# The latents' two norms and their split in one stage, and the final norm taken into the second block's first projection

## The reference, cut to what matters

```
def rmsnorm(x, g):
    xf = x.astype(F32)
    y = xf * lax.rsqrt(jnp.mean(xf * xf, axis=-1, keepdims=True) + RMS_EPS)
    return (y * g.astype(F32)).astype(x.dtype)

# the latent attention: two latents of 384 and 256 channels
qa, kva, kr = split(h @ mla_w_down)         # kva and kr for all 768 tokens
q  = rmsnorm(qa_lat, mla_q_norm) @ mla_w_uq      # 512 tokens
kv = rmsnorm(kva, mla_kv_norm) @ mla_w_ukv       # 768 tokens
...
# between the blocks
x = rmsnorm(x_lat, final_norm)              # end of the first block
h = rmsnorm(x, norm_mix_w_2)                # start of the second
proj = h @ w_in_2
...
x = x + merged @ w_out_2                    # x is used again here
```

## Time and profile before

| | |
|---|---|
| median of 3 runs | 3406.04 us |
| the profiled execution's own time | 3397.14 us |
| its span, first to last instruction | 3395.4 us |
| PE busy | 2957.6 us, 87% of the span |
| DVE busy | 1685.6 us, 50% |
| ACT busy | 1222.3 us, 36% |
| mean granted TensorE clock | 0.934 of full |

### The profile page before, as it was taken

How to read it: one execution, slowest core, us unless ns; L and a number is a source line. 1 busy time by engine, 2 the same in 40 slices (tenths; PEclk the granted TensorE clock), 3 DMA queues, 4 the chain that set the end, 5 groups by cost and what they waited for, 6 DMA issues and landing times. The chain is left out here.

```text
span 3395.4 us, 37900 instructions
## 1 busy us (share of the span) xinstructions
PE 2957.6 (87%) x14151; PEld 2324.7 (68%) x14151; DVE 1685.6 (50%) x2322; ACT 1222.3 (36%) x1630; POOL 164.6 (5%) x131
## 2 busy tenths in 40 slices
PE   6898998799999999867999999979757878599996
PEld 2384586687888888745777887757635567477775
DVE  1344432734767443435644433342466453588886
ACT  0321131423232232433424442244324322377774
POOL 0000000200011000000000000000000100212110
PEclk9999998899999999989999999989869788799998
DMA  6510010021345242110012222123100023599986
GB/s 245 194 50 13 32 44 26 1 87 67 123 145 170 71 137 93 38 39 21 1 48 89 93 93 75 62 75 93 44 0 1 1 68 131 187 351 349 348 335 238
DMA packets 76310, 362.77 MB, mean 107 GB/s; under 512 B 13428, under 2 KB 17347, under 8 KB 50596
## 3 DMA queue, kind: packets, MB, share of 16 engines
q1 hardware_dynamic: 62404, 327.69, 27.2%
q0 software_dynamic: 13792, 33.58, 3.0%
HBM read 360.68 MB, written 16.27 MB: 111 GB/s over the span
## 5 line engine op out<-in xcount | busy, mean ns | idle before, releaser
L305 PE MATMUL ps<-rounded,rounded 128*128 128x512 f32 (+3 forms) x3700 | 1377.2, 372 | 134.6 <-DVE rounded L2033 24.1
L306 PE MATMUL ps<-rounded,rounded 128*128 128x512 f32 (+3 forms) x3700 | 1338.0, 362 | 0.0
L307 PE MATMUL ps<-rounded,rounded 128*128 128x512 f32 (+3 forms) x3700 | 1335.4, 361 | 0.0
L305 PEld LDWEIGHTS ps<-rounded,rounded 128*128 128x128 f32 (+1 forms) x3700 | 706.4, 191 | 310.6 <-issue 100.0
L307 PEld LDWEIGHTS ps<-rounded,rounded 128*128 128x128 f32 (+1 forms) x3700 | 707.1, 191 | 107.5
L306 PEld LDWEIGHTS ps<-rounded,rounded 128*128 128x128 f32 (+1 forms) x3700 | 708.2, 191 | 95.2
L284 DVE TENSOR_TENSOR rounded<-work,rounded 128x1024 fp32r<-128x1024 f32 (+3 forms) x224 | 306.4, 1370 | 839.4 <-ACT rounded L280 839.3
L280 ACT CAST rounded<-work 128x1024 fp32r<-128x1024 f32 (+3 forms) x224 | 260.9, 1166 | 728.3 <-PE ps L307 640.2
L3181 DVE TENSOR_TENSOR rounded<-work,rounded 128x2048 fp32r<-128x2048 f32 x138 | 311.7, 2288 | 92.8 <-ACT rounded L3029 90.3
L3029 ACT CAST rounded<-work 128x2048 fp32r<-128x2048 f32 x138 | 258.5, 1908 | 85.5 <-PE ps L307 85.5
L291 PE MATMUL ps<-cst 128*128 128x256 f32 x432 | 122.3, 446 | 83.7 <-PEq L171 83.7
(11 more groups left out here) (439 smaller groups left out, 2545.7 us busy)
## 6 DMA issues: line engine op xcount, KB each, us to landing
work<-in_moe SPq DMA_DIRECT2D x138, 1024.0 KB, 7.3
work<-in_ffn_up SPq DMA_DIRECT2D x44, 1024.0 KB, 4.8
work<-in_ffn_down SPq DMA_DIRECT2D x66, 512.0 KB, 3.3
work<-in_ada_w SPq DMA_DIRECT2D x12, 2048.0 KB, 8.7
work<-in_ada_w POOLq DMA_DIRECT2D x48, 512.0 KB, 4.1
work<-in_w_out SPq DMA_DIRECT2D x16, 512.0 KB, 3.6
work<-in_w_gates SPq DMA_DIRECT2D x16, 512.0 KB, 3.6
work<-in_w_in_hy SPq DMA_DIRECT2D x12, 512.0 KB, 3.3
```

Source lines behind the costliest of these rows:

```text
L305: k.nc.tensor.matmul(out, sh, mh, start=start, stop=False)
L306: k.nc.tensor.matmul(out, sh, ml, start=False, stop=False)
L307: return k.nc.tensor.matmul(out, sl, mh, start=False, stop=stop)
```

## The change

`normalise` is gone. `latent_norms` does both latents' norms and their split in one stage, with the method of `Norm`: squares on ACT, tile sums on DVE, column sums on PE, two short roots (128x4 and 128x6), one short reciprocal, 10 diagonals, 10 spreading matmuls. Scaling and gain are one DVE instruction (line 692 of the new kernel), the high parts follow on ACT, and the low parts follow on DVE after all scaling.

`NormOfNorm` replaces the step `final` and the `Norm` of the `w_qk_2` projection. From one pass over `x` it makes two sums, of the squares of x and of the squares of x times the final gain; the first gives the final norm's inverse root, and the second times that inverse squared gives the mean square that the second norm needs. Each tile is scaled once by the product of both inverses. When the last low part is made, DVE writes the 8 tiles of `x` (normalised by the final norm alone, which the residual of the second block needs), and only then comes to the low parts of the next weights. The PSUM rooms of the norms inside `project_act` move: the sums from bank 6 to bank 3 and the matmuls of `keep_running` from bank 7 to bank 0.

```diff
+class NormOfNorm(Norm):
...
+        self.weighted = k.h
+        self.second_columns = sums_at[:, 8:8 + self.n]
+        self.first_inverse, self.mean = (k.made[:, at:at + self.n] for at in (16, 24))
+        self.first_diagonal = k.h_top[:, DT - 2, :]
...
+    def square(self, act):
+        for kk in range(DT):
+            self.k.nc.scalar.activation(self.part(self.squares, kk), self.part(self.k.x, kk), ACT.Square).then_inc(self.squared, 1)
+            self.k.nc.scalar.activation(self.part(self.weighted, kk), self.part(self.k.x, kk), ACT.Square,
+                                        scale=self.first_gain(kk)).then_inc(self.squared, 1)
+
+    def add(self, dve):
+        self.totals = self.part(self.squares, 0), self.part(self.weighted, 0)
+        for kk in range(1, DT):
+            dve.wait_ge(self.squared, 2 * kk + 2)
+            if kk > 1:
+                dve.wait_ge(self.added, 2 * kk - 2)
+            for total, squares in zip(self.totals, (self.squares, self.weighted)):
+                self.k.nc.vector.tensor_tensor(total, total, self.part(squares, kk), ALU.add).then_inc(self.added, 1)
...
+    def sum_and_spread(self, pe):
+        keep_running(k, 20, self.spare)
+        pe.wait_ge(self.added, 2 * DT - 2)
+        for squares, columns in ((self.squares, self.columns), (self.weighted, self.second_columns)):
+            for a in range(self.n):
+                last = k.nc.tensor.matmul(columns[:, a:a + 1], self.part(squares, 0)[:, a * P:a * P + P], k.cst[:, ONE:ONE + 1],
+                                          start=True, stop=True)
+        last.then_inc(self.summed, 1)
+        keep_running(k, 6, self.spare)
+        for n, (spread, diagonal) in enumerate(((self.spread, self.diagonal), (self.first_spread, self.first_diagonal))):
+            for a in range(self.n):
...
+                at = self.t0 + a * P
+                k.nc.tensor.matmul(spread[:, at:at + P], k.cst[:, ONE:ONE + 1].to_broadcast([P, P]), diagonal[:, at:at + P],
+                                   start=True, stop=True).then_inc(self.spread_done, 1)
+        keep_running(k, 4, self.spare)
...
+    def shift(self, act):
...
+        act.wait_ge(self.summed, 1)
+        k.nc.scalar.activation(self.root, self.columns, ACT.Sqrt, bias=k.const("eps"), scale=1.0 / D).then_inc(self.rooted, 1)
+        act.wait_ge(self.mean_made, 1)
+        k.nc.scalar.activation(self.root, self.mean, ACT.Sqrt, bias=k.const("eps"), scale=1.0 / D).then_inc(self.second_rooted, 1)
...
+    def scale(self, dve):
...
+        dve.wait_ge(self.rooted, 1)
+        link(V.reciprocal(self.first_inverse, self.root))
+        link(V.tensor_tensor(self.mean, self.second_columns, self.first_inverse, ALU.mult))
+        V.tensor_tensor(self.mean, self.mean, self.first_inverse, ALU.mult).then_inc(self.mean_made, 1)
+        dve.wait_ge(self.second_rooted, 1)
+        link(V.reciprocal(self.inverse, self.root))
+        link(V.tensor_tensor(self.inverse, self.inverse, self.first_inverse, ALU.mult))
+        for diagonal, inverse in ((self.diagonal, self.inverse), (self.first_diagonal, self.first_inverse)):
+            for a in range(self.n):
+                at = self.t0 + a * P
+                V.tensor_scalar(diagonal[:, at:at + P], k.const("ident"), inverse[:, a:a + 1], None, ALU.mult).then_inc(self.drawn, 1)
+        dve.wait_ge(self.spread_done, 2 * self.n)
+
+        def scale(kk):
+            if kk < DT:
+                V.scalar_tensor_tensor(out=self.part(k.h, kk), in0=self.part(k.x, kk), scalar=self.first_gain(kk),
+                                       in1=self.spread[:, self.t0:T], op0=ALU.mult, op1=ALU.mult).then_inc(self.scaled, 1)
+
+        scale(0)
+        scale(1)
+        for kk in range(DT):
+            dve.wait_ge(self.rounded, kk + 1)
+            V.tensor_tensor(self.part(k.h_pair.low, kk), self.part(k.h, kk), self.part(k.h_pair.high_plain, kk),
+                            ALU.subtract).then_inc(self.ready, 1)
+            scale(kk + 2)
+        dve.wait_ge(self.scaled, DT)
+        for kk in range(DT):
+            x = self.part(k.x, kk)
+            V.scalar_tensor_tensor(out=x, in0=x, scalar=self.first_gain(kk), in1=self.first_spread[:, self.t0:T],
+                                   op0=ALU.mult, op1=ALU.mult).then_inc(self.kept, 1)
+
+
+def latent_norms(k, x, norms):
...
+        def _(pe):
+            keep_running(k, 12, 6)
+            done = 0
+            for tiles, t0, count, at, gain, pair, spread in todo:
+                done += len(tiles) - 1
+                pe.wait_ge(added, done)
+                for a in range(count):
+                    last = nc.tensor.matmul(sums[:, at + a:at + a + 1], squares[:, tiles[0], t0 + a * P:t0 + a * P + P],
+                                            k.cst[:, ONE:ONE + 1], start=True, stop=True)
+                last.then_inc(summed, 1)
+            keep_running(k, 3, 6)
+            for tiles, t0, count, at, gain, pair, spread in todo:
+                for a in range(count):
+                    pe.wait_ge(drawn, at + a + 1)
+                    last = nc.tensor.matmul(spread[:, t0 + a * P:t0 + a * P + P], k.cst[:, ONE:ONE + 1].to_broadcast([P, P]),
+                                            diagonal[:, (at + a) * P:(at + a + 1) * P], start=True, stop=True)
+                last.then_inc(spread_done, 1)
+            keep_running(k, 12, 6)
+
+        @block.scalar
...
+                for n in tiles:
+                    nc.scalar.activation(squares[:, n, t0:T], x[:, n, t0:T], ACT.Square).then_inc(squared, 1)
+            for m, (tiles, t0, count, at, *_) in enumerate(todo):
+                act.wait_ge(summed, len(todo))
+                nc.scalar.activation(root[:, at:at + count], sums[:, at:at + count], ACT.Sqrt, bias=k.const("eps"),
+                                     scale=1.0 / (P * len(tiles))).then_inc(rooted, 1)
+            done = 0
+            for tiles, t0, count, at, gain, pair, spread in todo:
...
+        def _(dve):
+            seen = adds = 0
+            for tiles, t0, *_ in todo:
+                total = squares[:, tiles[0], t0:T]
+                for j, n in enumerate(tiles):
+                    seen += 1
+                    if j:
+                        dve.wait_ge(squared, seen)
+                        if j > 1:
+                            dve.wait_ge(added, adds)
+                        V.tensor_tensor(total, total, squares[:, n, t0:T], ALU.add).then_inc(added, 1)
+                        adds += 1
+            dve.wait_ge(rooted, len(todo))
+            V.reciprocal(inverse, root).then_inc(inverted, 1)
+            dve.wait_ge(inverted, 1)
+            for a in range(columns):
+                V.tensor_scalar(diagonal[:, a * P:(a + 1) * P], k.const("ident"), inverse[:, a:a + 1], None,
+                                ALU.mult).then_inc(drawn, 1)
+            parts = []
+            for m, (tiles, t0, count, at, gain, pair, spread) in enumerate(todo):
+                dve.wait_ge(spread_done, m + 1)
+                for j, n in enumerate(tiles):
+                    V.scalar_tensor_tensor(out=x[:, n, t0:T], in0=x[:, n, t0:T], scalar=gain(j), in1=spread[:, t0:T],
+                                           op0=ALU.mult, op1=ALU.mult).then_inc(scaled, 1)
+                    parts.append((pair, j, n, t0))
+            for done, (pair, j, n, t0) in enumerate(parts):
+                span = slice(t0 - pair.shift, T - pair.shift)
+                dve.wait_ge(rounded, done + 1)
+                V.tensor_tensor(pair.low[:, j, span], x[:, n, t0:T], pair.high_plain[:, j, span], ALU.subtract)
+
...
-def normalise(k, gain_of, shift_of, segs, dst=None, x=None, kt=DT, root_of=D, pair=None):
...
-def project_act(k, weights, dst, func, bias, segs, kt=DT, x=None, norm=None, then=None):
+def project_act(k, weights, dst, func, bias, segs, kt=DT, x=None, norm=None, then=None, first_norm=False):
...
-    norm = Norm(k, *norm, segs, k.pair(2), k.bank(6), 7) if norm else None
+    if norm:
+        kind, more = (NormOfNorm, (k.pair(3),)) if first_norm else (Norm, ())
+        norm = kind(k, *norm, segs, k.pair(2), k.bank(3), 0, *more)
     x = k.h_pair if x is None else x
...
-    normalise(k, lambda n, c: k.col("mla_q_norm", n), None, SEG_LAT, low, low, kt=3, root_of=Q_RANK)
-    normalise(k, lambda n, c: k.col("mla_kv_norm", n), None, SEGS, low[:, 3:5, :], low[:, 3:5, :], kt=2, root_of=KV_RANK)
-    split(k, [(low[:, n, CTX:T], qa.high[:, n, :], qa.high_plain[:, n, :], qa.low[:, n, :]) for n in range(3)]
-          + whole_tiles(kva, [low[:, 3 + n, :] for n in range(2)]))
+    latent_norms(k, low, (((0, 1, 2), SEG_LAT, lambda n: k.col("mla_q_norm", n), qa),
+                          ((3, 4), SEGS, lambda n: k.col("mla_kv_norm", n), kva)))
     project_act(k, "mla_w_qr", qr_plain, ACT.Identity, None, SEG_LAT, 3, qa)
...
     w_z, w_gates, w_xbc = (Stream(k, name, D, ahead=True) for name in ("w_z_2", "w_gates_2", "w_xbc_2"))
```

(40 more changed lines are left out.)

64 lines of the change are left out of this document (17 added, 47 removed).

## The result

The changed kernel took 3367.4 us (median of four runs, 3360.2 to 3375.7); beside it the kernel before took 3405.6 (3404.4 to 3407.0). The ratio is 0.9889, 95% interval 0.9863 to 0.9914: 38 us less. Forecast were 28.5 less, 3377.5 with a range of 3371 to 3386.

The account below looks back on a forecast made before the run. PE was taken to stand idle in two stretches, around the latents' norms and the final norm, behind engine waits and barriers. Savings of 14.9 and 13.6 us sum to 28.5, off the median 3406.04: 3377.5, range 3371 to 3386.

Parts of the forecast that it names:

- latents' stage: Three stages of the latents' norms, 32.5 us, become one of 18.7 at full clock: 13.8 us less.
- last of the 14 additions ends, from the stage's start: Stage of w_qk_2: DVE's seven pairs of tile sums end 12.3 us in, adding 2.5 us before the column sums.
- sums to first scaling: Stage of w_qk_2: 6 keep_running and eight spreads on PE take 5.0 us where it was 2.1: +2.9.
- pace and writes of `x`, to the third tile: Stage of w_qk_2: DVE's pace over 8 tiles +0.4, writes of x delaying the third tile's weights +0.4.
- final norm, residual to third tile: The final step's 20.75 us go and the w_qk_2 stage grows by 7.1: 13.6 us less.
- by that rule: Final norm: if signals behind each instruction cost nothing, the 14 additions take 8.5 us and the step gives 14.8.
- The last step: Whole kernel: the 28.5 us computed on the profiled execution of 3397.14 is taken off the median of 3406.04, giving 3377.5.
- My test for failure: Forecast wrong as a whole if the two stretches shrink under 20 us together or a far stage changes by over 2.
- the runs' spread at +-1.5: Whole kernel: part of the main forecast's band of 3374 to 3381, beside the adds, pace and short-instruction chain at +-1.
- half clock in the new waits: Both new stages: PE's fillers and spreads run at half clock, 5.6 us less gain, 3383; chance 0.14.
- half clock through the tiles of `w_qk_2`: Slower rival: six tiles of w_qk_2 at half clock instead of 5.46 us each, +32.8, 3410; chance 0.02.
- More than I count: Additions and 6 keep_running overlap better and stages behind start warm: 7 us more gain, 3370.5; chance 0.05.

Follow-up runs that it names:

- f1: Kernel before with extra keep_running at four places, ahead of both attentions and behind one first-mixer projection, covering short PE waits; 0.9965 of the kernel before, 3394.7 us.
- f2: Changed kernel with extra keep_running at four places, ahead of both attentions and behind one first-mixer projection; 0.9885 of the kernel before, 3371.8 us.
- e3: Changed kernel with the latents' three old stages put back, so the final norm's change alone; 0.9937 of the kernel before, 3387.7 us.
- f4: Changed kernel without the 12 keep_running that open the latents' stage; one execution, 3364.1 us.
- g3: Changed kernel with 2 keep_running (0.85 us) added ahead of one token tile of mla_w_v1; 0.9887 of the kernel before.
- g4: Changed kernel with 4 keep_running (1.7 us) added ahead of one token tile of mla_w_v1; 0.9904 of the kernel before.
- aa_before: Kernel before, unchanged, run against itself; 0.9997, median 3405.6 us, 12 runs from 3395 to 3409.
- e1_after: Changed kernel, unchanged, run again in more rounds against the kernel before; 0.9893, 3370.4 us.

## Why the prediction missed

**What held.** The bound and the mechanism of the two stretches did: both gave what they lost off the end. By the terms, with the first profiles:

| step | forecast | measured |
|---|---|---|
| latents, 24 records of `keep_running` | 5.5 | 5.42 |
| ten column sums | 2.4 | 2.29 |
| latents' stage | 18.7 | 18.0 (18.0 to 19.3 in seven profiles) |
| last of the 14 additions ends, from the stage's start | 12.3 | 12.3 (2185.82 to 2198.09) |
| eight column sums instead of four | +0.95 | +1.0 (1.95 and 0.95) |
| sums to first scaling | +2.9 | +2.4 (4.5 and 2.1) |
| pace and writes of `x`, to the third tile | +0.8 | +0.3 (15.96 and 15.64) |
| `load` stage | 0 | +0.6 (4.37 and 3.78) |
| final norm, residual to third tile | -13.6 | -13.9 |

The first scaling waited for PE's line 562, not for the diagonals, and PE waited 0.41 for the third tile's weights, against 0.4 forecast. The additions kept the two paces that had been read from the rows, 0.61 us behind one without a wait and 0.79 where one waits for the pair before, which the merged row (9.69 for 14) hides. Cut to single records it reads:

```profile
2188.40 0.69 DVE L546 TENSOR_TENSOR h<-h 128x512 f32<-128x512 f32 x1 [7.16 <-ACT h L536]
2189.01 0.68 DVE L546 TENSOR_TENSOR h<-h 128x512 f32<-128x512 f32 x1
2189.80 0.69 DVE L546 TENSOR_TENSOR h<-h 128x512 f32<-128x512 f32 x1
```

The Trainium skill, "VectorE: DVE Perf Modes", section "The DRAIN you can't avoid", has a semaphore behind each of a row of instructions cost nothing. The rows agree: each of line 691's eight multiplications signals one too, and they start 0.61 apart. The prediction set that rule against the 0.78, which is the price of waiting for the one before and not of the signal, so its 8.5 us "by that rule" was no fair reading; its sum did not use it.

Over all profiles with the old stage (six) and the new with its lead (seven) the latents' stretch is 190.8 and 176.1 on average, 14.7 less against 14.9; the final norm's is 208.5 (six) and 196.3 (eight), 12.2 less against 13.6, since the clock falls behind its new wait in six of them. Together 27 of the 28.5 forecast. That the new latents' stage keeps the full clock, on which its 14.9 rested, held in two of these seven profiles; in the other five the clock fell for a part of it, which costs up to 1.3 us.

**What failed.** The last step: "It lies 8.9 us under the median of 3406.04; the difference is taken over to the median." I took the distance as a property of the kernel's runs, the same before and after. It was mostly a stage: the latent attention, 151.6 in the profiled execution and 160.0 in the second profile of the same kernel, because the clock falls behind a wait of 1.67 us far from the change. (Between these two profiles other stages differ by up to 2.3 us each, and these differences cancel.) In the kernel before the long form is, by its times, the usual one (49 of 66 runs are at 3400 or above). In the changed kernel it is rare (one of five profiles that do not cover this wait), and its median lies 3.4 over its profiled execution, not 8.9 over. If all of before's typical executions have the long form and none of the changed kernel's, the medians differ by the 27 of the stretches plus the 8.5 of the attention, 35.5; the last 2.7 are within the spread. That waits of this kind make the difference is shown by f1 and f2: with them covered, the kernel before loses 12 us and its spread, the changed kernel nothing. That it is this wait among the four places is read from the profiles, where the attention goes from 160.0 to 150.3. The term that the prediction left out was thus a price of about 8.5 us on the kernel before's usual execution, which the change mostly took away. And it was luck that both first profiles had the short attention, so that they could be compared term by term.

My test for failure, that a stage far from the two would change by more than 2, did not trip on the pair of first profiles, in which both attentions were the short kind: it took a second profile of the same kernel to see it. The bounds of the range had the same fault: they held the terms of the change and "the runs' spread at +-1.5", when the runs of the kernel before spread over 20 us.

Of the rivals, "half clock in the new waits" is real and comes in most executions that were profiled (3.4 us in f2, up to 1.3 in the latents' stage). The one that was slower, half clock through the tiles of `w_qk_2`, was in no profile: in five (e3, f2, f4, g3 and g4) the clock was at 0.50 for 3 to 7 us of them, and at full for the rest. "More than I count" (7 us more) named the gain's size nearly, with the wrong cause: nothing behind the stretches became faster than the kernel before could be; the kernel before was only more often slow.

## What to carry to other kernels

A profile is one execution. Where its own time lies away from the median by more than a fraction of the effect that is looked for, take a second profile of the same kernel and compare it stage by stage before a sum is added to the median: here one stage held 8.4 of 8.9 us. The same goes for what an experiment shows of one stage: 18.0 us in one profile and 19.3 in another of the same kernel is all that f4 seemed to show. A change is worth its terms plus what it does to the odds of such a stage. And covering a short PE wait ahead of a stage of small matmuls can be worth more than the wait: six records of filler, 1.46 us, took the place of all but 0.37 of a wait of 1.67 behind which 8.5 us had been lost.

## What the runs showed of the hardware

- The granted clock fell behind a wait of 1.67 us in one execution and not in another of the same program (aa_before and before), and behind one of 2.02 in f2. The Trainium skill, "TensorE: Matmul & The Clock Gate", section "HAM oscillation — how this bites in real kernels", names long idle gaps for it; in these traces short ones did it as well.
- Once down, it stayed down for some 24 us in the latent attention though PE was busy by its records (24.94 of 25 us), while in f4's latents' stage it was at full again within 13 us of the stage's start. The second attention of e1_after ran at 0.50 from 2487 to 2528, where the first profile of the changed kernel has 0.50 from 2485 to 2508, and it was 7 us longer:

```profile
2496.00:2499.00 3.00, 2.56 (x6) 2.10 (x7) 0.98 (x3) 1.28 (x1) 0.00 (x0) 0.50 0.00 0
...
2520.00:2523.00 3.00, 3.00 (x11) 2.16 (x10) 0.32 (x1) 0.88 (x3) 0.00 (x0) 0.50 0.00 0
```

- Fill of 0.85 or 1.7 us put into PE's path of the kernel before did not make it measurably slower (0.9993 and 0.9992, intervals of about 0.15% to each side).
